# Five matmuls over three PSUM banks in place of six over two, in the FFN products of a hybrid recurrent trunk

## What is computed

```
def _swiglu(x, w_gate, w_up, w_down):
    return (jax.nn.silu(x @ w_gate) * (x @ w_up)) @ w_down
...
def _layer(x, state, p):
    f = _swiglu(_rmsnorm(x, p['ffn1_norm_pre']), p['ffn1_w_gate'], p['ffn1_w_up'], p['ffn1_w_down'])
    x = x + (0.5 * _rmsnorm(f, p['ffn1_norm_post'])).astype(x.dtype)
    m, new_state = _token_mixer(_rmsnorm(x, p['mix_norm_pre']), *state, p)
    x = x + _rmsnorm(m, p['mix_norm_post']).astype(x.dtype)
    f = _swiglu(_rmsnorm(x, p['ffn2_norm_pre']), p['ffn2_w_gate'], p['ffn2_w_up'], p['ffn2_w_down'])
    x = x + (0.5 * _rmsnorm(f, p['ffn2_norm_post'])).astype(x.dtype)
    return x, new_state
```

## Time and profile before

| | |
|---|---|
| median of 3 runs | 3801.59 us (3799.52 to 3802.06) |
| the profiled execution's own time | 3801.82 us |
| its span, first to last instruction | 3799.8 us |
| TensorE busy | 3450.5 us, 91% of the span |
| mean granted TensorE clock | 0.932 of full |

### The profile page before, as it was taken

One profiled execution on the slowest core, in us unless ns is written; L12 is line 12 of the kernel. 1 busy time (PEld: TensorE's weight loads), 2 busy tenths in 40 slices (PEclk: granted clock), 3 DMA queues, 4 the chain that ended last, 5 costly groups with the idle time before them and its releaser, 6 DMA issues. The chain is left out here.

```text
span 3799.8 us, 68663 instructions
## 1 busy us (share of the span) xinstructions
PE 3450.5 (91%) x25494; PEld 3262.0 (86%) x25494; DVE 1306.9 (34%) x1895; ACT 745.7 (20%) x1228; POOL 1556.6 (41%) x948
## 2 busy tenths in 40 slices
PE   8999899887877998999899998998778789989997
PEld 7999799866747997999889997998667479979997
DVE  2220275366444222221022202763564442132201
ACT  2110222223103112110021102322231021121100
POOL 4555466200004653555445553662000046535553
PEclk9999999999758999999999999999996589999999
DMA  3222122000103231222132222220001122312221
GB/s 120 88 85 84 55 90 86 28 0 0 63 23 100 88 93 56 86 88 84 51 93 88 87 83 61 84 88 20 0 0 63 57 75 88 92 56 88 87 83 64
DMA packets 77404, 258.82 MB, mean 68 GB/s; under 512 B 8272, under 2 KB 10064, under 8 KB 76496
## 3 DMA queue, kind: packets, MB, share of 16 engines
q1 hardware_dynamic: 76976, 256.43, 22.0%
q10 hardware_dynamic: 288, 0.49, 0.0%
HBM read 242.31 MB, written 14.58 MB: 68 GB/s over the span
## 5 line engine op out<-in xcount | busy, mean ns | idle before, releaser
L427 PE MATMUL ps<-hh,wh 128*128 128x272 f32 x4896 | 1422.3, 291 | 58.2 <-DVE hl L1255 45.0
L429 PE MATMUL ps<-hh,wl 128*128 128x272 f32 x4896 | 1419.0, 290 | 0.0
L428 PE MATMUL ps<-hl,wh 128*128 128x272 f32 x4896 | 1414.1, 289 | 0.0
L391 POOL TENSOR_SCALAR wh<-raw 128x1024 fp32r<-128x1024 f32 (+2 forms) x472 | 489.4, 1037 | 2141.8 <-PE ps L429 1220.9
L393 POOL TENSOR_TENSOR wl<-raw,wh 128x1024 fp32r<-128x1024 f32 (+2 forms) x472 | 1067.3, 2261 | 71.9 <-POOL wh L391 3.6
L427 PEld LDWEIGHTS ps<-hh,wh 128*128 128x128 f32 x4896 | 927.4, 189 | 69.5 <-issue 68.8
L428 PEld LDWEIGHTS ps<-hl,wh 128*128 128x128 f32 x4896 | 931.1, 190 | 0.0
L429 PEld LDWEIGHTS ps<-hh,wl 128*128 128x128 f32 x4896 | 928.3, 190 | 0.0
L427 PE MATMUL ps<-ah,wh 128*128 128x272 f32 x1408 | 410.2, 291 | 0.0
L429 PE MATMUL ps<-ah,wl 128*128 128x272 f32 x1408 | 405.8, 288 | 0.0
L428 PE MATMUL ps<-al,wh 128*128 128x272 f32 x1408 | 404.1, 287 | 0.0
(11 more groups left out here) (303 smaller groups left out, 3854.4 us busy)
## 6 DMA issues: line engine op xcount, KB each, us to landing
raw<-in_up SPq DMA_DIRECT2D x176, 512.0 KB, 3.6
raw<-in_win SPq DMA_DIRECT2D x80, 512.0 KB, 3.6
raw<-in_merge SPq DMA_DIRECT2D x96, 384.0 KB, 3.1
raw<-in_down SPq DMA_DIRECT2D x64, 512.0 KB, 3.5
raw<-in_down SPq DMA_DIRECT2D x32, 384.0 KB, 3.1
raw<-in_wout SPq DMA_DIRECT2D x16, 512.0 KB, 3.6
states<-in_in_gdn SPq DMA_DIRECT2D x2, 2048.0 KB, 8.3
proj<-in_in_ssd SPq DMA_DIRECT2D x2, 2048.0 KB, 15.7
```

The source lines that it names most:

```text
L391: pool.tensor_scalar(hi, src, 1.0, 1.0, MULT, MULT).then_inc(hi_done, 1)
L427: pe.matmul(out, wh[:, j % SPLIT, k, :], mh_[:, c], start=a, stop=False)
L428: pe.matmul(out, wh[:, j % SPLIT, k, :], ml_[:, c], start=False, stop=False)
L429: last = pe.matmul(out, wl[:, j % SPLIT, k, :], mh_[:, c], start=False, stop=b)
```

## The change

In the FFNs alone, a feature tile's high and low parts now lie in one row of 2·544 columns (`hx`, `ax`), arranged for each half h as: the first `NEAR` = 90 low columns, then all 272 high columns (together `WIDE` = 362); after both halves come the remaining 182 low columns of each (`FAR` = 182, together 364). Per k tile there are five matmuls: `wh` by each 362-column stretch into banks 0 and 1 of a slot, `wh` by the 364-column stretch into bank 2, and `wl` by the 272 high columns of each half, added onto the high part of banks 0 and 1. The columns streamed are the same, 362+362+364+272+272 = 1632 = 6·272. High and low results now lie apart in PSUM and are added by VectorE (`join`, three reductions over pairs).

- A slot is three banks, and there are two of them. The joined up result goes to banks 6 and 7 (`pair(3)`), the joined gate result to `sil`, where Silu now runs in place; the joined down results go to `f`, and ScalarE squares from there. The copy of `f` by ScalarE falls away in the FFNs.
- TensorE waits, before a gate or up block, for the join of the block two before it (`gate_whole`, `up_whole`); before, with four slots, it waited for Silu or `prod` of the pair before.
- The low part is written by two subtractions (90 and 182 columns of each half) in place of one.
- In `products`, which the mixer goes on using, the same six matmuls stand in another order: both halves of each kind, kind by kind.
- Some semaphores are merged to make room for two new ones; the instructions behind them stay.

```diff
+NEAR = 90
+FAR = HALF - NEAR
+WIDE = HALF + NEAR
...
+        hx, ax = row("hx", 0, [P, KD, 2 * T], F32R), row("ax", 16, [P, KF, 2 * T], F32R)
...
+        def join(eng, slot, dst):
+
+            flat = ps[:, :, :].rearrange("p b c -> p (b c)")
+            near = ps[:, 3 * slot:3 * slot + 2, 0:2 * NEAR].rearrange("p a (e t) -> p a t e", e=2)
+            eng.reduce_sum(dst[:, :, 0:NEAR], near, axis=mybir.AxisListType.X)
+            for h in range(2):
+                a = (3 * slot + h) * 512 + 2 * NEAR
+                apart = (3 * slot + 2) * 512 + h * FAR - a
+                both_ = flat[:, a:a + 2 * apart].rearrange("p (e t) -> p t e", e=2)[:, 0:FAR, :]
+                last = eng.reduce_sum(dst[:, h, NEAR:HALF], both_, axis=mybir.AxisListType.X)
+            return last
...
-                    for h in range(2):
-                        out = ps[:, 2 * slot + h, 0:HALF]
-                        c = slice(h * HALF, (h + 1) * HALF)
-                        a, b = start and n == 0, stop and n == len(ks) - 1
+                    a, b = start and n == 0, stop and n == len(ks) - 1
+                    halves_of = [(ps[:, 2 * slot + h, 0:HALF], slice(h * HALF, (h + 1) * HALF)) for h in range(2)]
+                    for out, c in halves_of:
                         pe.matmul(out, wh[:, j % SPLIT, k, :], mh_[:, c], start=a, stop=False)
+                    for out, c in halves_of:
                         pe.matmul(out, wh[:, j % SPLIT, k, :], ml_[:, c], start=False, stop=False)
+                    for out, c in halves_of:
                         last = pe.matmul(out, wl[:, j % SPLIT, k, :], mh_[:, c], start=False, stop=b)
...
+            def wide_product(layer, first, i, j, per, slot, nk, moving, start=True, stop=True, ready=None):
...
+                pe.wait_ge(lo_done, value(pe, layer * BLOCKS + i * per + (first + j + 1 + RAW)))
+                for k in range(nk):
...
+                    flat, w = moving(k), wh[:, j % SPLIT, k, :]
+                    a, b = start and k == 0, stop and k == nk - 1
+                    def high(h):
+                        return pe.matmul(ps[:, 3 * slot + h, 0:WIDE], w, flat[:, h * WIDE:(h + 1) * WIDE], start=a, stop=b,
+                                         skip_group_check=True)
+
+                    def far():
+                        return pe.matmul(ps[:, 3 * slot + 2, 0:2 * FAR], w, flat[:, 2 * WIDE:2 * T], start=a, stop=b,
+                                         skip_group_check=True)
+
+                    def low(h):
+                        return pe.matmul(ps[:, 3 * slot + h, NEAR:WIDE], wl[:, j % SPLIT, k, :],
+                                         flat[:, h * WIDE + NEAR:(h + 1) * WIDE], start=False, stop=False,
+                                         skip_group_check=True)
+
+                    if a:
+                        high(0), high(1), low(0), far()
+                        last = low(1)
+                    else:
+                        low(0), far(), low(1), high(0)
+                        last = high(1)
+                last.then_inc(blk_done, 1)
...
-                        pe.wait_ge(prod_done if j % 2 else sil_done, value(pe, layer * (2 * KF) + i * 2 + (which * KF + j // 2 + 1)))
-                        product(layer, first, i, j, 4, j, KD, h_tiles,
+                        pe.wait_ge(up_whole if j % 2 else gate_whole, value(pe, layer * (2 * KF) + i * 2 + (which * KF + j // 2 + 2)))
+                        wide_product(layer, first, i, j, 4, j % 2, KD, lambda k: hx[:, k, :],
...
-                        act.activation(halves(sil[:, j, :]), pair(2 * j), ACT.Silu).then_inc(sil_done, 1)
+                        act.wait_ge(gate_whole, value(act, n + 1 + 2))
+                        act.activation(sil[:, j, :], sil[:, j, :], ACT.Silu).then_inc(sil_done, 1)
...
+            def low_part(flat, whole):
+
+                high = high_of(flat).bitcast(F32)
+                dve.tensor_tensor(near_of(flat), halves(whole)[:, :, 0:NEAR], high[:, :, 0:NEAR], SUB)
+                return dve.tensor_tensor(far_of(flat), halves(whole)[:, :, NEAR:HALF], high[:, :, NEAR:HALF], SUB)
...
+                        dve.wait_ge(blk_done, value(dve, layer * BLOCKS + i * 4 + (first + 2 * j + 1 + SPLIT)))
+                        dve.wait_ge(prod_done, further(dve, n + 1))
+                        join(dve, 0, halves(sil[:, j, :])).then_inc(gate_whole, 1)
                         dve.wait_ge(blk_done, value(dve, layer * BLOCKS + i * 4 + (first + 2 * j + 2 + SPLIT)))
+                        dve.wait_ge(prod_done, further(dve, n + 2))
+                        join(dve, 1, pair(3)).then_inc(up_whole, 1)
+                        dve.wait_ge(up_whole, value(dve, n + 1 + 2))
                         dve.wait_ge(sil_done, further(dve, n + 3))
-                        dve.tensor_tensor(halves(prod[:, j, :]), halves(sil[:, j, :]), pair(2 * j + 1), MULT).then_inc(prod_done, 1)
+                        dve.tensor_tensor(halves(prod[:, j, :]), halves(sil[:, j, :]), pair(3), MULT).then_inc(prod_done, 1)
...
+                with dve.Fori(0, 2) as i:
+                    for m in range(4):
+                        dve.wait_ge(blk_done, value(dve, layer * BLOCKS + i * 12 + (first + UPS + 3 * m + 3 + SPLIT)))
+                        join(dve, m % 2, f[:, bass.ds(i * 4 + m, 1), :].rearrange("p k (a t) -> p (k a) t", a=2)).then_inc(out_done, 1)
```

More of the change, by code:

```diff
@@ L257, in trunk @@
         out_done = sem("out_done")
+        gate_whole, up_whole = sem("gate_whole"), sem("up_whole")
         evict_done, small_done = sem("evict_done"), sem("small_done")
@@ L266, in trunk @@
         l_ = {s: sem("l_" + s) for s in (
[L267 removed]
+            "rc z zt a g1 gk b bt qk qe dl d1 d2 ml at cp vc vtp vt kdp kt o oc ve su sm s").split()}
         s_ = {s: sem("s_" + s) for s in (
@@ L465, in pre_stats, with reduce_out @@
                 last.then_inc(sum_ready, 1)
-            def reduce_out(layer, stage, first, nks, moving, ready):
+            def reduce_out(layer, stage, first, nks, moving, ready, multiply):
                 per = len(nks)
@@ L476, in turn @@
                         for b, nk in enumerate(nks):
-                            product(layer, first, i, per * m + b, 4 * per, m % 2, nk,
-                                    lambda k, b=b: moving(k0[b] + k), b == 0, b == per - 1,
-                                    ready=(lambda k, b=b: ready(k0[b] + k)) if i is FIRST and m == 0 else None)
+                            multiply(layer, first, i, per * m + b, 4 * per, m % 2, nk,
+                                     lambda k, b=b: moving(k0[b] + k), b == 0, b == per - 1,
+                                     ready=(lambda k, b=b: ready(k0[b] + k)) if i is FIRST and m == 0 else None)
                         if i is FIRST and m == 0:
@@ L510, in ready @@
                     if k == 0:
-                        pe.wait_ge(sil_done, further(pe, layer * (2 * KF) + (which * KF + KF - 1 + 2)))
-                reduce_out(layer, 4 * which + 1, first + UPS, DOWN_K, lambda k: (ah[:, k, :], al[:, k, :]), ready)
+                        pe.wait_ge(gate_whole, further(pe, layer * (2 * KF) + (which * KF + KF + 2)))
+                reduce_out(layer, 4 * which + 1, first + UPS, DOWN_K, lambda k: ax[:, k, :], ready, wide_product)
             def common(step):
@@ L937, in split_h @@
                     act.wait_ge(hf_ready, value(act, layer * (4 * KD) + (number * KD + k + 1)))
-                    act.activation(hh[:, k, :], hf[:, k, :], ACT.Copy).then_inc(hh_ready, 1)
+                    act.activation(high_of(hx[:, k, :]) if number in (0, 3) else halves(hh[:, k, :]), halves(hf[:, k, :]),
+                                   ACT.Copy).then_inc(hh_ready, 1)
             def pre_norm(layer, stage, number):
@@ L950, in reduce_out @@
                     for m in range(4):
-                        act.wait_ge(blk_done, value(act, layer * BLOCKS + i * (4 * per) + (first + per * m + per + SPLIT)))
-                        act.activation(sq[:, m, :].rearrange("p (a t) -> p a t", a=2), pair(m % 2), ACT.Square).then_inc(sq_ready, 1)
-                        act.activation(f[:, bass.ds(i * 4 + m, 1), :].rearrange("p k (a t) -> p (k a) t", a=2),
-                                       pair(m % 2), ACT.Copy).then_inc(out_done, 1)
+                        if stage == 3:
+                            act.wait_ge(blk_done, value(act, layer * BLOCKS + i * (4 * per) + (first + per * m + per + SPLIT)))
+                        else:
+                            act.wait_ge(out_done, value(act, layer * (3 * KD) + i * 4 + (stage // 2 * KD + m + 1 + SPLIT)))
+                        whole = f[:, bass.ds(i * 4 + m, 1), :].rearrange("p k (a t) -> p (k a) t", a=2)
+                        act.activation(halves(sq[:, m, :]), pair(m % 2) if stage == 3 else whole, ACT.Square).then_inc(sq_ready, 1)
+                        if stage == 3:
+                            act.activation(whole, pair(m % 2), ACT.Copy).then_inc(out_done, 1)
```

(3 more changed lines are left out.)

51 lines of the change are left out of this document (30 added, 21 removed).

## The result

| | before | after |
|---|---|---|
| median | 3800.34 us (3798.76 to 3802.06, 20 runs) | 3807.76 us (3805.87 to 3814.4, 20 runs) |
| the profiled execution's own time | 3801.82 us | 3807.43 us |
| its span | 3799.8 us | 3805.6 us |

What follows compares the result with a forecast made beforehand. The prediction took TensorE to bound the kernel, paced by weight loads. From 3801.8 us it took 80.9 for the matmuls and added 3.2 for FFN begins and 4.8 for ends: 3729 us, range 3684 to 3800.

Steps and rivals of the forecast that it cites:

- What bounds the kernel: Whole kernel: TensorE, busy 91% of the span, is what the others wait for; FFNs last as long as its 2112 k tiles.
- The weight load sets the pace: TensorE at 272 columns: the next weight load takes 125 ns beside a full-speed stream, and the following matmul waits for it.
- −80.9 us: FFN matmuls: five in place of six gain 38.9 ns a k tile over 2080 k tiles; best −118.1 us, worst nothing.
- The three readings: TensorE's pace: no excess at half clock, some 3 ns in plain fp32, loads 0.11 us apart alone, 0.12 to 0.13 beside streams.
- the third rival: FFN matmuls: the excess goes with the columns, 0.46 ns each, so 3804 to 3810 us; chance 0.10.
- The range: Whole kernel: time expected between 3684 and 3800 us, leaving out some 0.19 of the chance.
- The join: VectorE in the FFNs: three reductions of 0.54 us, 1.63 us a join, costing nothing in the up stage.
- The down joins but the last: Down stages: these VectorE joins cost nothing, since a down tile lasts 15.7 us.
- End of an FFN: From last matmul to the logarithm: 3.63 us in place of 2.45, +1.2 us each, four times +4.8 us.
- Begin of an FFN: First block, paced by VectorE: the low part in two pieces adds 0.8 us, four times +3.2 us (bounds 2.4 and 5.9).
- The new order: `products` for the mixer's 8160 matmuls: same widths and loads, so nothing; 1 ns off either way would be 8 us.
- The VectorE bound: Up stage: VectorE becomes the bound from 1.2 us a reduction; about 4230 us if one costs what `al` does; chance 0.05.

Runs made afterwards that it cites:

- experiments 1 and 2: Kernel before plus series of 48 equal matmuls behind its last instruction, first by width and format, then by step and start; executions took 3941.67 and 3920.51 us.
- experiment 1: Kernel before plus series of 48 equal matmuls of several widths and formats behind its last instruction; 3941.67 us with the series, 125.4 ns per 272-column fp32r matmul.
- experiment 6: Changed kernel with the fourth down tile's sum of squares moved behind the fifth tile's blocks; 3794.70 us, ratio 0.9986.
- experiment 4: Changed kernel with `products` back in its old order, leaving the five matmuls and joins; 3814.02 us, ratio 1.0035.

## Why the prediction was wrong

- **What bounds the kernel**: right for the blocks. TensorE's pace sets their length before and after; it never waits for `gate_whole` or `up_whole`, and GpSimd isn't late. VectorE is late only in each FFN's first block, as forecast, and where a square follows a join.
- **"The weight load sets the pace"**: this step failed, and with it −80.9 us. The long matmuls took 167 ns, not 154, and the gain per k tile was 0 in place of 38.9 ns. The 12 ns above one column a cycle belong to the columns (experiments 1 and 2). The three readings that carried the picture were right and fit the rival one as well, which the forecast didn't work out: at half clock a four-byte stream asks for 4·272/227 = 4.8 bytes per ns, plain fp32 for 4·272/230 = 4.7, both far under the 8.7 that was reached. And the loads, 120 to 130 ns behind each other, were spaced by the matmuls, not the reverse: in experiment 1 they are as far apart as the matmuls at every width. The reading of 0.11 us for a load by itself stands; its extension to "125 ns beside a full-speed stream" was an assumption. The bound "the 12.0 ns belong to the columns and nothing is gained" stood there with 0.10 as a rival, put low because of the loads' spacing and because the Trainium skill's rule of the gap (TensorE: Matmul & The Clock Gate, Back-to-back issue gap) gives 115.8 ns for 272 columns. That rule fits bf16; the row of this kernel (125.3) already showed that it didn't hold here, and that should have counted for the third rival, not against it.
- **The range** ended at 3800, just under the rival that came true. It was cut there to leave out 0.19, though all the rest of the sum hung on one price that no row showed.
- **The join**: right. 1.43 us (forecast 1.63), reductions at 0.53 to 0.54 us as forecast, beside GpSimd too. The Trainium skill (SBUF — State Buffer, Who interferes with whom) says that a reduction on trn2 never contends with GpSimd. The trace agrees, though every join reads PSUM only and none tests a reduction that reads SBUF: 88 reductions from PSUM to PSUM, all beside GpSimd's rounding, take 542 ns in the mean. (Group by line: busy us, mean ns, idle before.)

```profile
L265 DVE TENSOR_REDUCE ps<-ps 128x180 f32<-128x360 f32 x88 | 47.7, 542 | 399.9 <-issue 202.1 <-PE ps L478 197.8
```

- **"The down joins but the last" cost nothing "since a down tile lasts 15.7 us"**: wrong, by 4·1.73 = 6.9 us. It looked at the VectorE work of a tile and not at the turn of the loop, where TensorE waits at once for the square of the tile that it has just finished (experiment 6: −7.6 us in the down stages without that).
- **End of an FFN**, 3.63 us in place of 2.45: right. From the last join's start to `rstd_post` it is 3786.35 − 3782.69 = 3.66 us:

```profile
3782.69 0.53 DVE L265 TENSOR_REDUCE f<-ps 128x360 f32 x1 [16.01 <-PE ps L478]
3783.14 0.97 DVE L270 TENSOR_REDUCE f<-ps 128x364 f32 x2
...
3784.30 0.66 ACT L1018 ACTIVATE sq<-f 128x544 f32 x1 [16.78 <-DVE f L270]
3784.97 1.28 ACT L989 ACT_TABLE_LOAD   x1
3786.35 0.62 ACT L991 ACTIVATE rstd_post<-ps 128x544 f32<-128x544 f32 x1
```

- **Begin of an FFN**, +3.2 us: right in kind, too large. It is +1.9 us, under the lower bound of 2.4: a tile of `hf` takes 1.40 us now in place of 1.33. Last FFN, from VectorE's first `hf` to GpSimd's start on the third block, which tells that the first block ended, before (12.60 us) and after (13.08), the same within 0.02 us in all four FFNs:

```profile
3368.10 1.48 DVE L1249 SCALAR_TENSOR_TENSOR hf<-x,prm,rstd 128x544 f32<-128x544 f32 x2 [9.04 <-ACT rstd L933]
3380.70 1.05 POOL L391 TENSOR_SCALAR wh<-raw 128x1024 fp32r<-128x1024 f32 x1 [32.71 <-PE ps L429]
...
3370.41 1.48 DVE L1316 SCALAR_TENSOR_TENSOR hf<-x,prm,rstd 128x544 f32<-128x544 f32 x2 [8.12 <-ACT rstd L993]
3383.49 1.04 POOL L420 TENSOR_SCALAR wh<-raw 128x1024 fp32r<-128x1024 f32 x1 [32.26 <-PE ps L478]
```

- **The new order, "nothing", bound 8 us**: the value was wrong, the bound held. It gives 6.3 us back, and without it the change would be 0.35% slower rather than 0.2%.
- **The VectorE bound** (4230 us) didn't come: a reduction costs 0.54, not the 1.2 us from which it decides.

The sum as it should have been, first without the new order: 3801.8 + 0 (matmuls) + 6.9 (middle waits) + 4.8 (ends) + 1.9 (begins) = 3815.4 us, against 3815.1 in the profiled execution of experiment 4, whose time at half clock is that of the kernel before. With the order's −6.3 it is 3809.1, against 3807.4. The 1.7 us between them aren't resolved; the time at half clock, 536.1 us in all for 518.0, differs there.

## What to carry to other kernels

Before counting on fewer, longer matmuls, divide the pace by the columns and ask for a second width: if the surplus is per column, fewer and longer matmuls save nothing, and a pace that is hidden at half clock says only that some rate is the limit, not which. A reading supports a picture only where the rival picture, worked out on the same row, gives another number. When a step is put between a result and the engine that sums it, look at the turns of the loops, where the next wait comes at once, and not only at the middle of a tile.

## What the runs showed of the hardware that was not expected

- A four-byte moving stream doesn't run at one column a cycle on full clock: 125.4 ns for 272 columns, 233.1 for 512, where bf16 takes 116.0 and 215.8. Two-byte elements with a step come to some 9 bytes swept per ns and partition, too (226.6 ns for 512, where side by side takes 215.8). That accounts for a part of what four-byte elements pay, not for all.
- Narrow fp32r matmuls aren't paid by the column: 64 and 192 columns took 112 ns alike at full clock, and 128 and 192 took 213 alike at half clock.
- The same six matmuls take 0.8 ns less each when the halves alternate (124.7 against 125.5). Over 20832 matmuls that is worth 17 us, while dropping 2112 of them won nothing.
- Over the versions here the mixer's projection stage lasts 713.6 to 720.4 us, its time at half clock 200 to 210 us, though none of them changes the recurrence in it. Differences of a few us between versions of this kernel can come from there.
